# A hybrid decoder trunk on one core: the second scores of a sparse attention step moved three places forward on TensorE, and exponentials and weighting put ahead of a weight split on ScalarE

## The reference

```python
n = rms(h); z = n @ W_in
A = conv_module(z_conv) @ P_A          # gated, causal depthwise conv of width 31, LayerNorm, silu
B = spatial_gating(z_sgu) @ P_B
C = sparse_attention(z_q, z_kv) @ P_C  # 8 heads in 2 groups, 64 wide; three softmaxes
h = h + W_out(sig(g_A) * A + sig(g_B) * B + sig(g_C) * C)
```

## Time and profile before

| | |
|---|---|
| median of 3 runs | 2709.38 us (2707.04 to 2709.95) |
| the profiled execution | 2714.68 us, its span 2712.8 us |
| mean granted clock of TensorE | 0.994 |
| TensorE busy | 2655.0 us, 98% of the span |
| VectorE, ScalarE, GpSimd busy | 48%, 40%, 45% |

### The profile page before, as it was taken

One profiled execution on the slowest core, in us unless ns is written; L12 is line 12 of the kernel. 1 busy time (PEld: TensorE's weight loads), 2 busy tenths in 40 slices (PEclk: granted clock), 3 DMA queues, 4 the chain that ended last, 5 costly groups with the idle time before them and its releaser, 6 DMA issues.

```text
span 2712.8 us, 36859 instructions
## 1 busy us (share of the span) xinstructions
PE 2655.0 (98%) x13092; PEld 2131.5 (79%) x13092; DVE 1314.7 (48%) x1828; ACT 1088.9 (40%) x1658; POOL 1233.5 (45%) x616
## 2 busy tenths in 40 slices
PE   7999999989999999999999999999899999999999
PEld 6888888866678868888888888887567788788887
DVE  5222259776535545252541213788764354543533
ACT  5322242446644454222342223424575445542222
POOL 4444456762235425444544435578422354344443
PEclk9999999999999999999999999999999999999999
DMA  4334433321234313333333353423112332233332
GB/s 129 99 95 117 116 97 94 74 56 50 59 82 117 101 47 108 97 97 96 91 101 94 100 129 97 107 78 74 51 51 59 98 113 86 63 101 101 93 101 78
DMA packets 487754, 243.90 MB, mean 90 GB/s; under 512 B 49501, under 2 KB 483015, under 8 KB 487623
## 3 DMA queue, kind: packets, MB, share of 16 engines
q1 hardware_dynamic: 487104, 242.02, 32.0%
q10 hardware_dynamic: 518, 0.13, 0.0%
HBM read 239.99 MB, written 2.10 MB: 89 GB/s over the span
## 4 chain that ended last, share of the span: by engine, by line
PE 68%; issue 16%; POOL 8%; DVE 5%; ACT 3%; DVEq 1%; ACTq 0%; POOLq 0%
PE pg L654 20%; PE pg L657 20%; PE pg L660 20%; POOL wL L603 8%; PE pA L748 2%; DVE convb L1767 1%; PE pA L935 1%; PE pA L882 1%; PE pg L680 1%; PE pA L810 1%; PE pg L681 1%; PE pg L682 1%; DVE prob L1933 0%; ACT prob L1178 0%; ACT wH L1178 0%
## 5 line engine op out<-in xcount | busy, mean ns | idle before, releaser
L603 POOL TENSOR_TENSOR wL<-raw,wH 128x1024 fp32r<-128x1024 f32 (+1 forms) x472 | 1090.6, 2312 | 1445.8 <-ACT wH L1178 1442.4
L654 PE MATMUL pg<-gxH,wH 128*128 128x512 f32 (+1 forms) x2384 | 930.2, 390 | 4.7 <-DVE gxL L1626 4.2
L660 PE MATMUL pg<-gxH,wL 128*128 128x512 f32 (+1 forms) x2384 | 923.4, 387 | 0.0
L657 PE MATMUL pg<-gxL,wH 128*128 128x512 f32 (+1 forms) x2384 | 917.6, 385 | 0.0
L1178 ACT ACTIVATE wH<-raw 128x1024 fp32r<-128x1024 f32 (+1 forms) x472 | 476.1, 1009 | 873.2 <-PE pg L660 695.1
L654 PEld LDWEIGHTS pg<-gxH,wH 128*128 128x128 f32 x2384 | 448.4, 188 | 106.9 <-issue 15.9
L660 PEld LDWEIGHTS pg<-gxH,wL 128*128 128x128 f32 x2384 | 448.5, 188 | 90.6 <-issue 3.9
L657 PEld LDWEIGHTS pg<-gxL,wH 128*128 128x128 f32 x2384 | 448.6, 188 | 89.5 <-issue 4.7
L654 PE MATMUL pg<-hH,wH 128*128 128x512 f32 x992 | 392.0, 395 | 4.3 <-POOL wL L603 2.7
L660 PE MATMUL pg<-hH,wL 128*128 128x512 f32 x992 | 394.2, 397 | 0.0
L657 PE MATMUL pg<-hL,wH 128*128 128x512 f32 x992 | 391.4, 395 | 0.0
(11 more groups left out here) (247 smaller groups left out, 2236.3 us busy)
## 6 DMA issues: line engine op xcount, KB each, us to landing
raw<-in_ffn_wi SPq DMA_DIRECT2D x352, 256.0 KB, 3.1
raw<-in_w_in SPq DMA_DIRECT2D x200, 256.0 KB, 3.2
raw<-in_ffn_wo SPq DMA_DIRECT2D x128, 256.0 KB, 3.1
raw<-in_ffn_wo SPq DMA_DIRECT2D x64, 192.0 KB, 2.6
raw<-in_xkv SPq DMA_DIRECT2D x32, 256.0 KB, 3.1
raw<-in_w_out SPq DMA_DIRECT2D x32, 256.0 KB, 3.0
raw<-in_sgu_out SPq DMA_DIRECT2D x32, 128.0 KB, 2.3
raw<-in_conv_out SPq DMA_DIRECT2D x32, 128.0 KB, 2.3
```

What stands on the lines that cost most here:

```text
L603: pool.tensor_tensor(wL[:, s % 4, 0:n, :], raw[:, s % 2, 0:n, :], wH[:, s % 4, 0:n, :].bitcast(F32), ALU.subtract)\
L654: mm(o, wH[:, s, k, :], rh(k), start=(k == 0), stop=False)
L657: mm(o, wH[:, s, k, :], rl(k), start=False, stop=False)
L660: last = mm(o, wL[:, s, k, :], rh(k), start=False, stop=(k == kt - 1))
```

## The change

In `attention`, the scores of b = 1 move from place 8 to place 5. In ScalarE's step, the split for the gate unit (`ahead(l, gate_unit(i + 1))`) moves from ahead of `turned_out(i - 1, 2)` to behind `exps(i, 1)`, which moves ahead of `turned_out(i - 1, 3)`; and `turned_out(i - 1, 4)`, there in the steps with five groups only (1, 5, 9, 13), moves behind `weighted(i)`.

```diff
-                    elif p in (1, 8):
+                    elif p in (1, 5):
                         if i < NS:
-                            scores((i, p // 8))
+                            scores((i, p // 5))
...
-                    ahead(l, gate_unit(i + 1))
-                    for g in range(2, min(n, 4)):
+                    for g in range(2, min(n, 3)):
                         turned_out(i - 1, g)
                     if i < NS:
                         exps(i, 1)
+                    ahead(l, gate_unit(i + 1))
                     if i == 8:
                         conv_high(2)
-                    for g in range(4, n):
+                    for g in range(3, min(n, 4)):
                         turned_out(i - 1, g)
                     if i < NS:
                         weighted(i)
+                    for g in range(4, n):
+                        turned_out(i - 1, g)
                     merge_gate(i)
```

## The result

The changed kernel takes 2715.88 us (median of 7 runs, 2713.39 to 2719.84), the kernel before 2709.95 in the 7 runs beside it (2707.04 to 2715.75). The ratio is 1.0022, with a 95% interval from 1.0012 to 1.0032: 5.9 us slower, within 3.3 to 8.7. The forecast was 14.6 us slower. The sign held, and the measured time lies in the range, which was wide; the size was less than half of what the sum gave.

The account below looks back on a forecast made before the run. TensorE, busy 98% of the span, was taken as the bound, with 11 us of waits a layer to win. Terms summed to 7.4 us a layer, 14.8 in both, on 2709.4: 2724 us, range 2707 to 2732.

Parts of the forecast that it names:

- step 5: At place 5 of step 5, TensorE waits for VectorE to empty the b=0 score banks: 1.25 us a layer.
- Step 11: At place 5 of step 11, TensorE waits 2.1 us for the b=0 score banks; net 1.85 us a layer.
- change of kind: Scores away from the value matmuls cost TensorE 0.21 us more per step; 11 steps pay, 2.3 us a layer.
- Steps 7 and 8: ScalarE's new order makes step 7 net 0.4 us sooner and changes step 8 by 0.
- the long wait of step 1: TensorE's new 3.6 us wait for `turned_out(3)` in step 1, with 1.4 us of half clock, is absorbed.
- the clock after step 11: Step 11's 2.1 us wait drops TensorE's granted clock, adding 1.4 us a layer (bounds 0 and 1.4).
- the price of steps 1 to 3: What VectorE's chain moves in steps 1 to 3: between -2.6 and 1.5 us, taken as +0.5 a layer.
- `turned_out(3)`: In steps 3, 5, 9, 13 its release for TensorE's transposes comes 0.2 to 0.4 us later: 0.5 us a layer.
- Rival 1: VectorE wins 2.6 us in steps 1 to 3 and the clock holds after step 11: 2715 us, chance 0.16.
- Rival 2: Waits at place 5 cost nothing; only changes of kind stay, less gains: about 2710 us, no change, chance 0.10.
- rival 3: ScalarE's order sets the long waits ahead of steps 2 and 3; the change removes them: 2705 or 2702.6 us, chance 0.11.
- Rival 4: Waits in steps 5 and 8 drop the clock too, steps 1 to 3 and 7 lose: 2734 us, chance 0.08.

## Why the prediction was off

**Right: the places.** Every wait stood where the prediction put it: 3.29 us in step 1 (forecast 3.6), none ahead of step 2, one still ahead of step 3, 0.86 us in step 5 (1.25), 1.96 in step 11 (2.1). Step 11 is 1.93 to 1.95 us longer, change of kind included (1.85 + 0.21). The change of kind cost 0.17 to 0.21 us in each of the six steps of the first layer with nothing else in them (0.21), though not for the reason that an excursion more is paid: what is lost is the company of the values. Steps 7 and 8 gave back 0.48 together (0.4), not by one wait gone and another as long as before, but by both becoming shorter (0.84 to 0.38 and 1.10 to 0.70). That the long wait of step 1 would be absorbed held too. No gate or branch matmul of these stretches waited for `wL`, as forecast.

**Wrong: the clock after step 11, the term of 1.4 us a layer.** It was 0 in both layers. The prediction argued that 2.1 us is longer than the 1.92 us that had brought the half clock twice. The wait was 1.96 us, also longer than 1.92, and the clock held. Two drops out of two at one length of wait were taken for a rule, and the runs show none: behind the six waits of step 11 between 1.96 and 1.99 us the clock fell once.

**Wrong: the price of steps 1 to 3, +0.5 us a layer.** They came out at -0.27 and -3.10. Two things were in it. First, VectorE's chain was taken as 0.5 us later, because each slide of GpSimd would meet another two-input operation; it came 0.6 sooner. From the first maxima of step 1 to the weighting of step 2 it took 21.58 us before (576.50 to 598.08) and 21.00 in the changed kernel (577.52 to 598.52). The two groups of four taps in step 2 won 1.93 and 1.13 us; the idle time ahead of the maxima took 1.37 of it, the `wv` product of step 2 0.94, and the two taps of step 1 0.17. The prediction had named the collision with the product for step 1, where it kept its 0.24 us, and not for step 2, and its bound of 1.2 us for the win left out the first group of taps, 5.98 us long. Second, the wait ahead of step 3, shorter by 2.35 us since TensorE comes to it later by its wait in step 1, dropped the clock once in two, where 4.20 us had dropped it both times. Step 3 took 19.73 us in the first layer, with the drop, and 18.15 in the second. Before, it took 21.75 and 22.92; in the second layer the clock stayed down longer (0.50 in 1940 to 1943 us and still 0.64 in the 3 us behind).

**Sized too high: step 5, and `turned_out(3)`.** Step 5 cost 1.21 us, where 1.25 + 0.21 for its change of kind + 0.15 for `turned_out(3)` was forecast. Steps 9 and 13 are 0.15 and 0.25 us longer in all, where 0.31 each was forecast: of the 0.1 for the later release little came.

The sum a layer, in us:

| term | forecast | layer 1, layer 2 |
|---|---|---|
| steps 1 to 3, with step 3's 0.13 and the change of kind in step 3 | +0.84 | -0.27, -3.10 |
| steps 4 to 15 without the clock | +5.2 | +4.20, +4.15 |
| clock after step 11 | +1.4 | 0, 0 |

Both layers: 14.8 forecast, 5.0 by the table. Of the difference of 9.8, steps 1 to 3 hold 5.1, the clock 2.8 and the waits 2.0 (rounded). Rival 1 (VectorE's gain and a clock that holds, 2715 us) comes nearest to what happened, and it had a chance of 0.16. Its clock held after step 11; its win of 2.6 us in steps 1 to 3 came in one layer of the changed kernel, and in both only with the split behind everything (3.5 and 4.7 us). Rival 2 and rival 3 are refuted above. Rival 4's further drops did not come: no wait under 1.7 us dropped the clock.

**The port.** In the earlier trace rows the trace had VectorE's taps standing still under GpSimd's split; here even a VectorE product on two tiles of 128x4 took 1.10 us in place of 0.16, in step 2 of both layers, when it met a split (and 1.00 or 1.01 in step 6); with the scores alone moved, and in the three kernels with a later split in step 2, it has 0.16 or 0.17. The Trainium skill (SBUF — State Buffer, Who interferes with whom) describes an exclusive lock between VectorE instructions with two SBUF inputs and GpSimd instructions that read SBUF. The traces agree: 1.10 us beside a split, 0.16 without.

## What to carry to other kernels

When an engine's order is changed so that one collision goes, follow the moved instruction to its new place and look at what the other engine runs there: here a split left four taps (1.13 us won) and cost a 128x4 product nearly as much (0.94), and only a third place, behind the weighting, with the scores where they had been, gave a gain of 8 us. An operand that is asked for three places earlier makes the consumer wait if its producer ends just in time; two steps of fifteen held three quarters of that cost, so such an order is to be priced step by step. A clock drop after a wait of some 2 us came in 9 of 24 cases here: price it by how often it happened at waits of that length, not as certain.

## What the runs showed of the hardware

**The granted clock after a wait.** Over all twelve kernels' traces (before, after, ten experiments), TensorE's waits in the attention parts by length, and how often the granted clock of the 3 us behind was 0.5 to 0.8 instead of 1.00:

| wait, us | waits | clock fell |
|---|---|---|
| 1.0 to 1.7 | 66 | 0 |
| 1.75 to 2.04 | 24 | 9 |
| 2.6 to 2.8 | 6 | 3 |
| 3.0 to 3.6 | 18 | 14 |
| 4.20 and 4.24 | 2 | 2 |

In the kernel with the scores at place 6, the same wait of 1.81 us ahead of step 3 left the clock at 1.00 in the first layer and brought 0.67 in the second:

```profile
600.00:603.00 3.00, 3.00 (x17) 1.00 0.00 0
...
1940.50:1943.50 3.00, 3.00 (x13) 0.67 0.00 0
```

A drop lengthened its own step by 1.3 to 1.6 us where another layer or kernel had the same step and wait without one (step 11: +3.47 against +1.95 us; step 8 with the scores alone: +2.57 against +0.99), and by 1.1 to 1.2 more where the clock stayed down longer (step 1 of the second layer with the scores at place 7 and at place 6). What decides it at waits between 1.75 and 3.6 us, these runs do not settle.

**Neighbours on TensorE.** Scores beside value matmuls save 0.2 us over the two apart; scores beside transposes save nothing (0.44 + 0.62 against 1.06 us).

**A split between VectorE and GpSimd.** Where GpSimd's split of the large tile ran beside four VectorE taps they took 5.98 us before and 6.11 in the first layer of the kernel with place 8 in steps 5 and 11; where it came behind them, 4.05 us.
